# Third column group of a gated ConvFFN in fp32: up and down as Strassen's seven products on halves of 184 columns

## The reference, cut to what matters

```python
def conv_ffn(h, conv_prev, lp):
    u = h @ lp['w_up']                      # 1024 -> 2 x 2816
    a, b = u[..., :D_FF], u[..., D_FF:]
    ext = jnp.concatenate([conv_prev.astype(a.dtype), a], axis=1)
    c = lp['conv_b'] + ext[:, 0:T] * lp['conv_w'][0]
    for j in range(1, CONV_W):
        c = c + ext[:, j:j + T] * lp['conv_w'][j]
    y = (jax.nn.gelu(c, approximate=False) * b) @ lp['w_down']   # 2816 -> 1024
    return y, ext[:, T:]
# x = x + conv_ffn(rms_norm(x, norm2_g)); then a final norm
```

## Time and profile before

| what | us |
|---|---|
| median of 3 runs | 2823.65 (2822.10 to 2825.14) |
| span of the profiled execution, first to last instruction | 2792.2 |
| median above that span (launch and end) | 31.4 |
| PE busy in the span | 2641.2 (95%) |
| FFN of group 2: up, 352 matmuls | 220.4 |
| FFN of group 2: down, 176 matmuls and 18 transposes | 110.6 |
| after the last matmul of down | 12.1 |

### The profile page before, as it was taken

One profiled execution on the slowest core, in us unless ns is written; L12 is line 12 of the kernel. 1 busy time (PEld: TensorE's weight loads), 2 busy tenths in 40 slices (PEclk: granted clock), 3 DMA queues, 4 the chain that ended last, 5 costly groups with the idle time before them and its releaser, 6 DMA issues. The chain is left out here.

```text
span 2792.2 us, 45329 instructions
## 1 busy us (share of the span) xinstructions
PE 2641.2 (95%) x18040; PEld 1637.6 (59%) x18040; DVE 1511.3 (54%) x2872; ACT 807.2 (29%) x1798; POOL 278.3 (10%) x321
## 2 busy tenths in 40 slices
PE   8998999999997977899799999999999999999998
PEld 5554566666654324788655666655656665656665
DVE  2115888865533447676569999877843222221111
ACT  2214322135434562111112331013335321144410
POOL 0000111000000000000001221001354430000000
PEclk9999999999998986999999999999999999999999
DMA  5101121231114340000243223344366543523332
GB/s 215 33 13 41 42 85 63 72 93 48 36 52 170 101 139 16 19 12 11 103 135 106 106 106 118 123 136 138 108 215 223 172 149 102 175 99 108 109 111 87
DMA packets 86770, 278.66 MB, mean 100 GB/s; under 512 B 18584, under 2 KB 43000, under 8 KB 74208
## 3 DMA queue, kind: packets, MB, share of 16 engines
q1 hardware_dynamic: 74528, 224.64, 23.6%
q0 software_dynamic: 12032, 51.14, 5.7%
...
## 5 line engine op out<-in xcount | busy, mean ns | idle before, releaser
L2104 PE MATMUL tl_P<-base,tl_WU 128*128 128x368 f32 x2112 | 663.0, 476 | 5.9 <-DVE base L2495 5.9
L2104 PEld LDWEIGHTS tl_P<-base,tl_WU 128*128 128x128 f32 x2112 | 402.8, 192 | 259.6 <-issue 13.8
L407 PE MATMUL dp_PS<-base,dp_W 128*128 128x368 f32 x1440 | 465.8, 476 | 0.0
L407 PEld LDWEIGHTS dp_PS<-base,dp_W 128*128 128x128 f32 x1440 | 265.8, 190 | 157.5 <-issue 8.8
L2120 PE MATMUL tl_P<-base,tl_WD 128*128 128x368 f32 x1056 | 333.1, 473 | 0.0
L2120 PEld LDWEIGHTS tl_P<-base,tl_WD 128*128 128x128 f32 x1056 | 198.6, 190 | 123.8 <-issue 4.1
L148 PE MATMUL pa_PG<-pa_W,base 128*128 128x402 f32 (+1 forms) x576 | 199.3, 506 | 7.6 <-DMA pa_W<-in_w_dsa 7.6
L706 DVE TENSOR_SCALAR_CACHE_REDUCE dp_EQ<-dp_SCORE,dp_trial 128x1024 f32<-128x1024 f32 (+1 forms) x186 | 175.9, 946 | 19.9 <-issue 1.1
L148 PEld LDWEIGHTS pa_PG<-pa_W,base 128*128 128x128 f32 (+1 forms) x576 | 107.2, 187 | 94.6 <-issue 14.5
L2436 DVE MAX8 tl_v<-arena 128x8 f32<-128x4100 f32 x32 | 141.8, 4432 | 3.4 <-issue 1.5
L2439 DVE FIND_INDEX8 tl_i<-tl_v,arena 128x8 uint32<-128x4100 f32 x32 | 141.5, 4423 | 0.0
...
## 6 DMA issues: line engine op xcount, KB each, us to landing
tl_WU<-in_wu SPq DMA_DIRECT2D x66, 1024.0 KB, 4.7
...
dp_W<-in_w_rw SPq DMA_DIRECT2D x15, 1024.0 KB, 4.8
...
```

The lines of the kernel that those rows point to most:

```text
L407: last = pe.matmul(bank(f)[:, 0:w], W[:, t // 2 % 2, k, 128 * (t % 2):128 * (t % 2) + 128], xT[:, k, c:c + w], start=k == 0, stop=k == KD - 1)
L2104: last = pe.matmul(out[:, 0:W], WU[:, i % 2, o:o + 128], XN[:, k, :], start=k == 0, stop=k == KD - 1)
```

## The change

For group 2 alone `up`, `down`, `read_a`, `read_b`, `conv_add`, `gate_up` and `add_down` are no longer called. In their place stand 34 blocks (`BLOCKS3`): 22 up blocks (f = 0 to 21) and 12 down blocks, in the order up 0 to 8, down chunk 0 (channel tiles 0 to 7) for the four pairs of output tiles, up 9 to 16, down chunk 1 (8 to 15), up 17 to 21, down chunk 2 (16 to 21). Each block is a 2x2 block product over halves of the contraction, two output tiles (`a` and `b` of one f, or two output tiles t) and halves of 184 columns, done as seven products (Strassen's, in Winograd's form): `block3` on PE, each product `depth` matmuls of 184 columns (4; in chunk 2 it is 3). Four of the seven use sums of weight tiles, made for each block (`weight_sum`: 0 and 2 on GpSimd, 1 and 3 on VectorE, 512 columns each), and four use sums of the moving halves: of the norm once (`mix_norm`, four sums of 736 columns), of the hidden tiles for every pair of f (the end of `multiply`, four sums of 184). The products go to four banks A, B, D, E, three of which take two products a block; ScalarE (`keep1`, `keep5`, `left_a`) and VectorE (`take2`, `take3`, `take_rest`) read them in between, and GpSimd makes the last sum of the right half (`right`).

The convolution now takes one scaled copy on ScalarE (`first_tap`) and two fused multiply-adds of 384 columns on VectorE (`convolve`); GpSimd copies the edges (`edge`, `keep_last`, two small copies each). On VectorE the order in a block n is: `convolve` and `multiply` of the up block before, `take2(n)`, in the last three blocks the gains and totals of the final norm, two weight sums for n + 1, `take3(n)`, `take_rest(n)`. Weights have three buffers (`load_block`). Of the 24 transposes of `last_turn`, six each stand before the last two blocks (where 18 stood in `down`), twelve in `last_rows`. The weights of `up` are laid out with all of `a` before all of `b`, for every group.

```diff
+CHUNKS = ((0, 8), (8, 16), (16, NF))
+BLOCKS3 = []
+for _c, (_lo, _hi) in enumerate(CHUNKS):
+    BLOCKS3 += [("up", _f) for _f in range(_lo + (_c > 0), _hi + (_hi < NF))] + [("down", _c, _p) for _p in range(4)]
 
...
+def weight_sum(eng, n, j):
+    raw, ws = raw_at(n), sums_at(n)
+    if j in (0, 2):
+        eng.wait_ge(raw_in[n % 3], 16 * (n // 3 + 1))
+        if n >= 2:
+            eng.wait_ge(d_made, 2 * n - 2)
+    else:
+        eng.wait_ge(sum_made[j // 2 if j == 1 else 1], n + 1)
+    if j == 0:
+        eng.tensor_tensor(ws[:, 0], raw[:, 2], raw[:, 3], ALU.add).then_inc(sum_made[0], 1)
+    if j == 1:
+        eng.tensor_tensor(ws[:, 1], ws[:, 0], raw[:, 0], ALU.subtract).then_inc(sum_made[1], 1)
+    if j == 2:
+        eng.tensor_tensor(ws[:, 2], raw[:, 0], raw[:, 2], ALU.subtract).then_inc(sum_made[2], 1)
+    if j == 3:
+        eng.tensor_tensor(ws[:, 3], raw[:, 1], ws[:, 1], ALU.subtract).then_inc(sum_made[3], 1)
 
...
+        def load_block(n):
+            if n < 2:
+                sp.wait_ge(b_done, 2 * NF - 1 + n)
+            elif n == 2:
+                sp.wait_ge(branched, 48)
+            else:
+                sp.wait_ge(d_made, 2 * n - 4)
+            what = BLOCKS3[n]
+            o = 0 if what[0] == "up" else down0[what[1]] + 512 * depth(n) * what[2]
+            src = I["wu"][:, what[1]] if what[0] == "up" else I["wq"][:, o:o + 512 * depth(n)]
+            sp.dma_start(RAW[n % 3][:, 0:512 * depth(n)], src).then_inc(raw_in[n % 3], 16)
 
...
+        def block3(n):
+            what, kk = BLOCKS3[n], depth(n)
+            raw, ws = raw_at(n), sums_at(n)
+            if what[0] == "up":
+                left = lambda k: XN[:, k, half[0]]
+                left2 = lambda k: XN[:, 4 + k, half[0]]
+                right2 = lambda k: XN[:, 4 + k, half[1]]
+                mix = lambda j: lambda k: TX[:, j, k, :]
+            else:
+                at = lambda e: lambda k: HB[:, (4 * what[1] + k) % 5, e, :]
+                left, left2, right2 = at(0), at(2), at(3)
+                mix = lambda j: at(4 + j)
+
+            def product(out, weights, moving, first):
+                for k in range(kk):
+                    if n == 0 and moving is left:
+                        pe.wait_ge(xn_done, 32 + k + 1)
+                    last = pe.matmul(out[:, 0:H], weights[:, k, :], moving(k), start=first and k == 0,
+                                     stop=k == kk - 1, skip_group_check=True)
+                return last
+
+            pe.wait_ge(raw_in[n % 3], 16 * (n // 3 + 1))
+            if what[0] == "down":
+                pe.wait_ge(multiplied, min(CHUNKS[what[1]][1], NF - 1))
+            pe.wait_ge(a_taken, 2 * n)
+            product(BANK_A, raw[:, 0], left, True).then_inc(a_made, 1)
+            if n == 0:
+                pe.wait_ge(tx_done, 2)
+            if what[0] == "down":
+                pe.wait_ge(pair_done, CHUNKS[what[1]][1] // 2)
+            pe.wait_ge(sum_made[1], n + 1)
+            pe.wait_ge(b_taken, 2 * n)
+            product(BANK_B, ws[:, 1], mix(1), True).then_inc(b_made, 1)
+            pe.wait_ge(sum_made[0], n + 1)
+            pe.wait_ge(d_taken, 2 * n)
+            product(BANK_D, ws[:, 0], mix(0), True).then_inc(d_made, 1)
+            pe.wait_ge(a_taken, 2 * n + 1)
+            product(BANK_A, raw[:, 1], left2, False).then_inc(a_made, 1)
+            if n == 0:
+                pe.wait_ge(tx_done, 4)
+            pe.wait_ge(sum_made[2], n + 1)
+            pe.wait_ge(b_taken, 2 * n + 1)
+            product(BANK_B, ws[:, 2], mix(2), False).then_inc(b_made, 1)
+            pe.wait_ge(e_taken, n)
+            product(BANK_E, raw[:, 3], mix(3), True).then_inc(e_made, 1)
+            pe.wait_ge(sum_made[3], n + 1)
+            pe.wait_ge(d_taken, 2 * n + 1)
+            product(BANK_D, ws[:, 3], right2, False).then_inc(d_made, 1)
 
...
-                        last.then_inc(last_turned, 1)
-            if g < 2:
-                sums(2 * g + 1, KD - 1)
+            sums(2 * g + 1, KD - 1)
+        for r in range(3):
+            pe.wait_ge(freed[r], uses[r])
+        pe.wait_ge(evacuated, TS)
+        for n in range(NBL):
+            block3(n)
+            if n == NBL - 3:
+                pe.wait_ge(expd, TS // 4)
+                pe.wait_ge(untiled, TS // 4)
+                pe.wait_ge(y_done, TS // 4)
+                pe.wait_ge(rooted, 5)
...
+        def keep1(n):
+            act.wait_ge(a_made, 2 * n + 1)
+            act.activation(part1[:, n % 2, :], BANK_A[:, 0:H], ACT.Copy).then_inc(a_taken, 1)
+
+        def keep5(n):
+            act.wait_ge(d_made, 2 * n + 1)
+            if n >= 2:
+                act.wait_ge(right_done, n - 1)
+            act.activation(part5[:, n % 2, :], BANK_D[:, 0:H], ACT.Copy).then_inc(d_taken, 1)
+
+        def left_a(n):
+            f = BLOCKS3[n][1]
+            act.wait_ge(a_made, 2 * n + 2)
+            if f >= 2:
+                act.wait_ge(conv3, f - 1)
+            act.activation(AA[:, f % 2, 2:2 + H], BANK_A[:, 0:H], ACT.Copy).then_inc(a_taken, 1)
+
+        def first_tap(f):
+            act.drain()
+            act.wait_ge(a_right, f + 1)
+            act.wait_ge(edged, f + 1)
+            if f >= 2:
+                act.wait_ge(multiplied, f - 1)
+            act.activation(CC[:, f % 2, :], AA[:, f % 2, 0:384], ACT.Identity, bias=cw[:, 3, f:f + 1],
+                           scale=cw[:, 0, f:f + 1]).then_inc(tapped, 1)
+
+        def curve3(f):
+            act.wait_ge(conv3, f + 1)
+            act.activation(CC[:, f % 2, :], CC[:, f % 2, :], ACT.Gelu).then_inc(curved3, 1)
+
         def open_gate(i):
...
+            keep1(n)
+            if before[0] == "up":
+                curve3(before[1])
+            if before[0:2] == ("down", 2):
+                for t in (2 * before[2], 2 * before[2] + 1):
+                    square(40 + t)
+                if n == NBL - 1:
                     act.activation(WARM[:, :], eps[:, :], ACT.Sqrt)
-            if g < 2:
-                root(2 * g + 1)
...
+        def edge(f):
+            if f >= 2:
+                pool.wait_ge(conv3, f - 1)
+            pool.tensor_copy(AA[:, f % 2, 0:2], AL[:, f, :])
+            pool.tensor_copy(AA[:, f % 2, 306:386].rearrange("p (b q) -> p b q", q=10)[:, :, 0:2],
+                             cst[:, f])
+            pool.drain().then_inc(edged, 1)
+
+        def keep_last(f):
+            pool.wait_ge(a_right, f + 1)
+            pool.tensor_copy(CL[:, f, 0, :], AA[:, f % 2, 304:306])
+            pool.tensor_copy(CL[:, f, 1:, :],
+                             AA[:, f % 2, 306:386].rearrange("p (b q) -> p b q", q=10)[:, :, 8:10])
+            pool.drain().then_inc(conv_last, 1)
+
+        def right(n):
+            what = BLOCKS3[n]
+            pool.wait_ge(b_taken, 2 * n + 2)
+            pool.wait_ge(d_taken, 2 * n + 1)
+            if what[0] == "up":
+                f = what[1]
+                if f >= 2:
+                    pool.wait_ge(multiplied, f - 1)
+                pool.tensor_tensor(BB[:, f % 2, half[1]], part3[:, n % 2, :], part5[:, n % 2, :], ALU.add)
+            else:
+                x = X1[:, 2 * what[2] + 1, half[1]]
+                pool.tensor_tensor(x, x, part3[:, n % 2, :], ALU.add)
+                pool.drain()
+                pool.tensor_tensor(x, x, part5[:, n % 2, :], ALU.add)
+            pool.drain().then_inc(right_done, 1)
+
+        for j in (0, 1, 3, 2):
+            weight_sum(pool, 0, j)
+        for n in range(NBL):
+            if n and BLOCKS3[n - 1][0] == "up":
+                keep_last(BLOCKS3[n - 1][1])
+            if BLOCKS3[n][0] == "up":
+                edge(BLOCKS3[n][1])
+            if n + 1 < NBL:
+                weight_sum(pool, n + 1, 0)
+                weight_sum(pool, n + 1, 2)
+            right(n)
 
     @block.vector
...
+        def mix_norm():
+            low, high = XN[:, 0:4], XN[:, 4:8]
+            dve.drain()
+            dve.tensor_tensor(TX[:, 0], low[:, :, half[1]], low[:, :, half[0]], ALU.subtract).then_inc(tx_done, 1)
+            dve.drain()
+            dve.tensor_tensor(TX[:, 1], high[:, :, half[1]], TX[:, 0], ALU.subtract).then_inc(tx_done, 1)
+            dve.tensor_tensor(TX[:, 2], high[:, :, half[1]], low[:, :, half[1]], ALU.subtract).then_inc(tx_done, 1)
+            dve.drain()
+            dve.tensor_tensor(TX[:, 3], high[:, :, half[0]], TX[:, 1], ALU.subtract).then_inc(tx_done, 1)
...
+        def convolve(f):
+            dve.wait_ge(tapped, f + 1)
+            for j in (1, 2):
+                dve.scalar_tensor_tensor(CC[:, f % 2, :], AA[:, f % 2, j:j + 384], cw[:, j, f:f + 1],
+                                         CC[:, f % 2, :], ALU.mult, ALU.add)
+                dve.drain()
+            dve.drain().then_inc(conv3, 1)
+
+        def multiply(n):
+            f = BLOCKS3[n][1]
+            q = f // 2
+            hb = HB[:, q % 5]
+            to = hb[:, 2 * (f % 2):2 * (f % 2) + 2, :].rearrange("p e n -> p (e n)")
```

(70 more changed lines are left out.)

147 lines of the change are left out of this document (101 added, 46 removed).

## The result

The kernel after takes 2843.39 us (median of 4, 2838.14 to 2846.65), before 2824.36 us in the same rounds: ratio 1.0067, 95% interval 1.0052 to 1.0081, slower by 19.0 us. The prediction was slower, 2840; the measured time lies in its range of 2806 to 2864.

A forecast was written before the change was run, and what follows sets the result against it. PE was taken to bound the kernel, busy 95% of the span. Terms -38.6 + 3.8 + 9.4 + 24.0 + 6.1 + 1.7 + 10.2 - 0.7 + 0.3 = +16.2 us on 2792.2, plus 31.4 above the span: 2840, range 2806 to 2864.

The forecast's parts named there:

- Products: Group 2's FFN on PE: 1848 records at 0.1557 us, 287.8 us for 326.3 removed, a gain of 38.6 us.
- rival D: PE's weight loads in the blocks are not hidden, by the skill's rule: +198 us, about 3038; chance 0.01.
- Rival E: Block products run at another pitch, moving halves being read from tiles 184 or 368 wide: 5 ns a record, 9 us.
- Start: First block: PE waits for the norm's tiles and sums and runs at half clock, 6.4 us lost against 2.6: +3.8.
- Even stalls: PE waits at product 5 for take2 behind each even f: eleven of 0.85 us, 9.4 us.
- Odd stalls: PE waits for take2 behind odd f, where four pair sums come first: ten of 2.4 us, 24.0 us.
- f = 21: First block of down chunk 2 waits for the last pair's sums after one product: 6.1 us.
- Clock: PE's clock falls to half behind six of ten odd stalls, 10.2 us, and behind the 6.1 us wait, 1.7.
- Rest: Fewer transposes before the end, -0.7 us; six transposes and a shorter add behind the last product, +0.3; DMA and layout nothing.
- rival A: GpSimd and VectorE do not hinder each other in the chain to take2: -16.6 us, 2807; chance 0.13, 0.17 with neighbours.
- Rival B: Waits in the blocks as predicted, but PE's clock holds: +6.0 us, 2829 to 2830; chance 0.24.
- rival C: GpSimd takes both sums before VectorE's turn and the clock falls at every odd stall: +39 us, 2863; chance 0.12.

The follow-up runs named there:

- a0: The changed kernel, unedited, profiled a second time and timed beside before in the same rounds: 2821.22 us against 2795.56, ratio 1.0087.
- e1: The changed kernel with take2(n) moved between convolve and multiply, except behind the last up tile: 2798.29 us, ratio 0.9918 to before.
- e2: The changed kernel with GpSimd's weight sums 0 and 2 made for 16 columns instead of 512: 2808.65 us, ratio 0.9950 to before.
- e3: The changed kernel with GpSimd's weight sum 0 of the next block ahead of keep_last and edge, sum 2 behind: ratio 1.0018 to before.

## Why the prediction was right

By its own steps, from the profile of after:

- **Products.** 0.1557 us a record was predicted from a line through two other widths (368 and 128 columns); 1735 of 1848 records are at 0.1558. Removed work: 38.5 us of 38.6. The weight loads, one of 128 columns for each record, are hidden (rival D, and the rule of the Trainium skill, "TensorE: Matmul & The Clock Gate", section "What overlaps and what doesn't", by which it would have been near 3038, are out). Rival E too.
- **Start.** From the end of `rows` to product 4 of block 0 11.0 us, where 24 records at full rate behind the 0.8 us of before end after 4.5: 6.5 lost, 6.4 predicted. That it fits so well is partly luck: it took 10.3 in a0, where the clock rose sooner, and 11.4 in e1. And I had missed a wait: PE stands 2.98 us for ScalarE's last copy of a finished row before product 1. It hid behind the norm's sums, for which product 2 waits anyway.
- **Even stalls.** 0.88 for 0.85; behind f = 8 and 16, where a down block follows and GpSimd comes to its sums without `edge`'s copies, 1.96 and 1.47, behind f = 20 0.34. Together 10.9 for 9.4.
- **Odd stalls.** 2.48 for 2.4, together 24.9 for 24.0. **f = 21:** 5.97 for 6.1.
- **Clock.** I took six falls of ten at 1.7 (10.2 us). There were three at 1.75 (5.2) in this execution and five (8.8) in the other; 1.5 for 1.7 behind f = 21. And the first record behind each of 18 stalls is 0.08 slow, 1.4 us that I did not have.
- **Rest.** -0.7 and +0.3, as predicted.

Sum: -38.5 + 3.9 + 10.9 + 24.9 + 6.0 + 5.2 + 1.5 + 1.4 - 0.7 + 0.3 = +14.9, and 15.0 measured; 16.2 was predicted. The clock's term was 5.0 us too large, nearly twice what it cost, and the terms of the stalls and of the slow first records were 3.8 too small (1.5, 0.9 and 1.4): that these nearly cancel is luck. The 19.0 us of the timed runs are probably these 15 and what the last part of other executions has more (a0: 19.1; of the four timed executions of after the two longest have a mean clock of 0.956, the others 0.959 and 0.960), give or take the scatter ahead of group 2. The timed executions have no trace, so this is not shown. The size was right because the odd stalls and the even ones were laid out instruction by instruction with turns between VectorE and GpSimd; rival A (no hindrance) is e2's kernel, and it is faster by 0.5%, as A said in kind (2807 forecast for it, 2808.65 measured; in the last part A's sum of -16.6 us stands against -12.5). Rival B, by which the clock holds, missed by three to five falls; in rival C GpSimd takes both sums before VectorE gets its turn, and 2.16 us for the two multiply-adds show that it doesn't.

Two inner numbers were wrong and met. GpSimd's sum of 512 columns takes 1.27 us where nothing meets it (sum 0 in e3: 1271 ns), not 1.18, and 1.36 and 1.49 here, with its waits for VectorE. The rows had it: the line 0.18 + 1.95 ns a column gives 0.90 us for 368 columns where the earlier trace rows has 965 ns, and a line through the 320 ns for 64 columns and these 965 gives 1.27 for 512. The stalls came out right all the same, since sum 0 starts 0.33 us behind the first multiply-add and not 0.55. And "2823.65 is 31.4 above the span for launch and end" was wrong: it is 1.8, and the rest was the difference between two executions, most of it in the stretch at the start of the gathers. It did not hurt, since the sum was made against one execution and the offset carried over whole.

Of the signs, PE's idle time (38 us, by `take2` and the pair's sums), its pattern by even and odd f and the pitch came as said. Two did not: the granted clock is 0.95 to 0.98 in the three up stretches, not under 0.9, and the second multiply-add takes 1.46 us in the block shown above, not near 1.1. The layout of the chain itself had 2.2 us for the two together, and 2.16 were measured.

What I did not see, although the layout of the chain had it, is that the worst term, 36 us of stalls, hung on the place of one 0.35 us instruction.
